# A two-block transformer forward on one core: an earlier query unit and halved ropes in mixer B, and narrow row sums for the norm ahead of the third FFN

## What is computed

```python
def mixer_b(h, cos16, sin16, w_in, sinks):
    q, k, v, q_mem = split_cols(h @ w_in, B_SPLITS)          # 1024, 256, 256, 256
    q = apply_partial_rope(q.reshape(B, S, 16, 64), cos16, sin16)
    k = apply_partial_rope(k.reshape(B, S, 4, 64), cos16, sin16)
    ...
    o, _ = banded_window_attention(q, k, v, 127, 64 ** -0.5, sink=sinks)
    return o.reshape(B, S, 1024), q_mem

# third layer, after its mixer
x = x + gt1 * rmsnorm_2(y, g_post1)
h2 = rmsnorm_2(x, g_pre2) * (1 + sc2) + sh2
x = x + gt2 * rmsnorm_2(conv_ffn(h2, ...), g_post2)
```

## Time and profile before

| what | value |
|---|---|
| median of 3 runs | 2167.69 us (2163.6 to 2168.49) |
| time of the profiled execution | 2167.15 us |
| its span in the trace | 2165.4 us |
| mean granted TensorE clock | 0.972 |
| mixer B: from the last projection matmul to the first output matmul | 827.0 to 967.9 us |
| post1 and pre2: from the last matmul of `c_out` to the first of `up20` | 1748.4 to 1783.1 us |

### The profile page before, as it was taken

The page is one execution under the profiler, slowest core; times in us unless marked ns, Lnnn a source line. Parts: engine busy times, 40 slices in busy tenths (PEclk is TensorE's granted clock), DMA queues, the critical chain, the costliest instruction groups (busy, mean ns, idle before and its releaser), DMA issues.

```text
span 2165.4 us, 25929 instructions
## 1 busy us (share of the span) xinstructions
PE 2001.3 (92%) x9702; PEld 1598.4 (74%) x9702; DVE 1122.4 (52%) x2007; ACT 670.7 (31%) x1058; POOL 871.2 (40%) x648
## 2 busy tenths in 40 slices
PE   3989789999999988989999999999999959999997
PEld 3766467788778776558788887788876848888886
DVE  7777874533943675754534534872233554312334
ACT  3233463321122124562321222234444222212211
POOL 4343103444744552105445544542221423444442
PEclk9999899999999999999999999999999979999998
DMA  4222001422532341003324422332110212223221
GB/s 159 78 79 97 25 1 63 165 98 73 209 136 91 139 150 59 25 23 110 117 91 149 160 97 104 104 105 76 59 59 20 98 57 79 85 80 117 97 80 66
DMA packets 32205, 199.14 MB, mean 92 GB/s; under 512 B 3696, under 2 KB 3824, under 8 KB 14320
## 3 DMA queue, kind: packets, MB, share of 16 engines
q1 hardware_dynamic: 27216, 166.74, 22.0%
q10 hardware_dynamic: 4896, 31.15, 4.0%
HBM read 195.78 MB, written 2.10 MB: 91 GB/s over the span
## 4 chain that ended last, share of the span: by engine, by line
PE 49%; DVE 4%; ACT 1%; POOL 1%; issue 1%; DVEq 0%; ACTq 0%
PE psum L1514 42%; PE psum L1536 2%; PE psum L1707 2%; PE psum L1689 1%; POOL w_lo L565 1%; PE psum L1672 1%; PE psum L1974 1%; DVE xT L1024 1%; DVE work L1018 1%; PE psum L1644 0%; ACT w_hi L595 0%; PE psum L1635 0%; DVE work L1029 0%; DVE h_lo L1008 0%; PE psum L1628 0%
## 5 line engine op out<-in xcount | busy, mean ns | idle before, releaser
L565 POOL TENSOR_TENSOR w_lo<-raw,w_hi 128x512 fp32r<-128x512 f32 (+2 forms) x640 | 862.7, 1376 | 1264.8 <-ACT w_hi L595 1264.8
L1514 PE MATMUL psum<-h_hi,w_hi 128*128 128x512 f32 x1560 | 614.2, 394 | 14.1 <-POOL w_lo L565 6.6
L1514 PE MATMUL psum<-h_hi,w_lo 128*128 128x512 f32 x1560 | 611.2, 392 | 0.0
L1514 PE MATMUL psum<-h_lo,w_hi 128*128 128x512 f32 x1560 | 610.5, 391 | 0.0
L595 ACT ACTIVATE w_hi<-raw 128x2048 fp32r<-128x2048 f32 (+3 forms) x177 | 301.6, 1704 | 565.7 <-PE psum L1514 474.4
L1514 PEld LDWEIGHTS psum<-h_hi,w_hi 128*128 128x128 f32 x1560 | 294.0, 188 | 87.4 <-issue 14.5
L1514 PEld LDWEIGHTS psum<-h_hi,w_lo 128*128 128x128 f32 x1560 | 293.7, 188 | 63.6 <-issue 2.4
L1514 PEld LDWEIGHTS psum<-h_lo,w_hi 128*128 128x128 f32 x1560 | 293.8, 188 | 62.2 <-issue 2.3
L1514 PE MATMUL psum<-g_hi,w_hi 128*128 128x512 f32 x528 | 207.6, 393 | 10.9 <-POOL w_lo L565 5.8
L1514 PE MATMUL psum<-g_hi,w_lo 128*128 128x512 f32 x528 | 205.6, 389 | 0.0
L1514 PE MATMUL psum<-g_lo,w_hi 128*128 128x512 f32 x528 | 205.6, 389 | 0.0
(11 more groups left out here) (312 smaller groups left out, 2424.1 us busy)
## 6 DMA issues: line engine op xcount, KB each, us to landing
raw<-w_up SPq DMA_DIRECT2D x66, 1024.0 KB, 4.8
raw<-w_dn SPq DMA_DIRECT2D x48, 704.0 KB, 4.1
mod_w<-w_mod ACTq DMA_DIRECT2D x24, 1024.0 KB, 4.9
raw<-w_c_in SPq DMA_DIRECT2D x13, 1024.0 KB, 4.9
raw<-w_b_in SPq DMA_DIRECT2D x7, 1024.0 KB, 4.9
raw<-w_a_idx SPq DMA_DIRECT2D x5, 1024.0 KB, 5.7
raw<-w_a_out SPq DMA_DIRECT2D x8, 640.0 KB, 3.9
raw<-w_b_out SPq DMA_DIRECT2D x8, 640.0 KB, 3.9
```

Of the source, the lines that this page charges most:

```text
L565: ins = nc.gpsimd.tensor_tensor(LO[slot][:, a:z], RAW[slot][:, a:z], HI[slot][:, a:z].bitcast(F32), ALU.subtract)
L1514: ins = nc.tensor.matmul(out, l, r, start=(k == 0 and m == 0), stop=(k == n - 1 and m == 2))
```

## The change

Mixer B: the unit of query tiles 0 and 1 comes second and the values third (the columns of the weight are laid out so). The start of attention on PE waits for keys and those two query tiles, no more for the values. At step 0 PE issues `AHEAD_B` = 12 filler matmuls ahead of the first transposes, and 6 a step from then on instead of 7; `b_finished` counts that. Ropes inside attention are halved: shuffle and times cosine in one step, times sine and add in the next. ACT evaluates one exponential before the projections, which brings its table in there.

Third FFN: `pre2` sums each square on PE with one moving column into banks 0 to 3, chunk by chunk, and puts its inverses into bank 5.

```diff
-          ("b_in", 7, 2048, [2, 4, 2, 2, 2, 2, 2]), ("b_out", 8, 1280, 1),
+          ("b_in", 7, 2048, [2, 2, 4, 2, 2, 2, 2]), ("b_out", 8, 1280, 1),
...
-        FILL_MEM, FILL_B, FILL_C, LAST_C = 12, 7, 40, 12
+        FILL_MEM, FILL_B, AHEAD_B, FILL_C, LAST_C = 12, 6, 12, 40, 12
+
+        def b_finished(k):
+
+            return (AHEAD_B + FILL_B * k) // 24 if k > 0 else 0
...
                 root, sums = T[:, 2, 0:rows], bank(norm_bank(name), 0, rows)
+                if name == "pre2":
+                    root, sums = ROOT[:], ps[:, 0:4 * S].rearrange("p (t n) -> p t n", n=S)[:, :, 0]
...
             for u in range(3):
                 next_hi(ph, u // 2, u % 2)
-                if u == 1:
+                if u == 0:
+                    nc.scalar.activation(WARM[:, 14:15], cst("eps"), ACT.Exp)
+                if u == 2:
                     for t in range(ROWT):
...
+                    elif name == "pre2":
+                        nc.vector.reciprocal(INV[:], ROOT[:]).then_inc(pre2_inverse, 1)
+                        v.wait_ge(pre2_spread, 1)
+                        inv = bank(5)
...
                 step(nc.vector.stream_shuffle(sw, src, mask))
+                if later:
+                    step(nc.vector.tensor_tensor(dst, src, cos[0:n, :], ALU.mult))
+
+                    def rest():
+                        step(nc.vector.tensor_tensor(sw, sw, sin[0:n, :], ALU.mult))
+                        nc.vector.tensor_tensor(dst, dst, sw, ALU.add).then_inc(done, 1)
+                    return rest
...
             def b_between(k):
-                for tile in range(min(finished(FILL_B, k - 1) if k else 0, 6), min(finished(FILL_B, k), 6)):
-                    b_tile(3 + tile // 2, tile % 2, BQ[:, 2 + tile, :], 5 + tile)
+                if begun:
+                    begun.pop()()
+                for tile in range(min(b_finished(k - 1), 6), min(b_finished(k), 6)):
+                    begun.append(b_tile(3 + tile // 2, tile % 2, BQ[:, 2 + tile, :], 5 + tile, later=True))
...
+                if name == "pre2":
+                    for t in range(ROWT):
+                        bank_free(t)
+                    for k in range(nch):
+                        pe.wait_ge(square_ready, b + k + 1)
+                        for t in range(ROWT):
+                            ins = nc.tensor.matmul(bank(t, 0, 1), T[:, k % 2, t * P:(t + 1) * P], ONES[:, 0:1],
+                                                   start=k == 0, stop=k == nch - 1)
+                        ins.then_inc(square_used, 1)
+                    bank_free(5)
+                    pe.wait_ge(pre2_inverse, 1)
+                    for t in range(ROWT):
+                        ins = nc.tensor.matmul(bank(5, t * P, (t + 1) * P), INV[:, t:t + 1].broadcast_to([P, P]),
+                                               cst("ident", P), start=True, stop=True)
+                    ins.then_inc(pre2_spread, 1)
...
-                if u == 1:
-                    last_read[4] = (scaled_ready, NORMS["mix1"][4] + DC)
+                if u == 2:
                     advance(r_tiles(ph, u, range(4), range(4, 8), 0, 256))
...
                     group = (k + 2) // 4
-                    if k % 4 == 2 and 2 <= group < 8:
+                    if k == 0:
+                        advance(rest, AHEAD_B)
+                    if k % 4 == 2 and group < 8:
                         pe.wait_ge(ph.free, 3 + group)
-                    elif k % 4 == 2 and group == 8:
-                        pe.wait_ge(qkv_ready, 15)
+                    elif k % 4 == 2 and group < 10:
+                        pe.wait_ge(qkv_ready, 6 + group)
                 else:
                     advance(rest, FILL_B)
-            pe.wait_ge(qkv_ready, 13)
-            pe.wait_ge(ph.free, 4)
+            pe.wait_ge(ph.free, 3)
```

More of the change, by code:

```diff
@@ L148, in lay_out @@
     bq = b[:, :1024].reshape(D, 16, 64)[:, pair16].reshape(D, 1024)
-    w["b_in"] = units(np.concatenate([b[:, 1024:1536], bq, b[:, 1536:]], 1), 256)
+    w["b_in"] = units(np.concatenate([b[:, 1024:1280], bq[:, :256], b[:, 1280:1536], bq[:, 256:], b[:, 1536:]], 1), 256)
     bo = x["b_w_out"][0]
@@ L370, in program @@
         final_inverse, final_spread = sem("final_inverse"), sem("final_spread")
+        pre2_inverse, pre2_spread = sem("pre2_inverse"), sem("pre2_spread")
         XR = {"final": 0, "post1": 8, "post2": 16}
@@ L882, in _ @@
                 next_hi(ph, u // 2, u % 2)
-                if u == 1:
+                if u == 0:
+                    nc.scalar.activation(WARM[:, 14:15], cst("eps"), ACT.Exp)
+                if u == 2:
                     for t in range(ROWT):
-                        act.wait_ge(ph.done, ph.before(1) + t + 1)
+                        act.wait_ge(ph.done, ph.before(2) + t + 1)
                         nc.scalar.activation(BV[:, t, :], bank(4 + t, 0, 256), ACT.Copy).then_inc(qkv_ready, 1)
@@ L889, in b_between @@
             def b_between(k):
-                for tile in range(min(finished(FILL_B, k - 1) if k else 0, 8), min(finished(FILL_B, k), 8)):
+                for tile in range(min(b_finished(k - 1), 8), min(b_finished(k), 8)):
                     if tile >= 6:
@@ L1039, in _, with rope @@
             ropes = []
-            def rope(src, dst, cos, sin, half, done, count, n=P, swapped=None, scale=1.0):
+            def rope(src, dst, cos, sin, half, done, count, n=P, swapped=None, scale=1.0, later=False):
                 if swapped == "bank":
@@ L1419, in _, with b_tile @@
             ph = PH["b_in"]
-            def b_tile(u, c, dst, count, scale=1.0):
+            def b_tile(u, c, dst, count, scale=1.0, later=False):
                 v.wait_ge(ph.done, ph.before(u) + c + 1)
-                rope(bank((u % 2) * 2 + c if u < 3 else c), dst, C16, S16, 8, ph.free, count, swapped=BSW, scale=scale)
+                return rope(bank(2 * u + c if u < 2 else c), dst, C16, S16, 8, ph.free, count, swapped=BSW, scale=scale, later=later)
             for c in range(2):
@@ L1427, in _ @@
             for c in range(2):
-                b_tile(2, c, BQ[:, c, :], c + 3)
+                b_tile(1, c, BQ[:, c, :], c + 3)
+            begun = []
             def b_between(k):
-                for tile in range(min(finished(FILL_B, k - 1) if k else 0, 6), min(finished(FILL_B, k), 6)):
-                    b_tile(3 + tile // 2, tile % 2, BQ[:, 2 + tile, :], 5 + tile)
+                if begun:
+                    begun.pop()()
+                for tile in range(min(b_finished(k - 1), 6), min(b_finished(k), 6)):
+                    begun.append(b_tile(3 + tile // 2, tile % 2, BQ[:, 2 + tile, :], 5 + tile, later=True))
             attend(b_all, b_between)
@@ L1613, in norm @@
                 i, nch, rows, b, s = NORMS[name]
+                if name == "pre2":
[13 more added lines that the diff above has]
+                    ins.then_inc(pre2_spread, 1)
+                    for t in range(ROWT):
+                        last_read[t] = (root_ready, i + 1)
+                    last_read[5] = (scaled_ready, s + nch)
+                    return
                 bank_free(norm_bank(name))
@@ L1864, in _ @@
                     advance(t_tiles(ph, u, (0, 1), (b, b + 1), ready=h_chunk("mix1") if u == 0 else None))
-                    last_read[b], last_read[b + 1] = (ph.free, u + 1), (ph.free, u + 2)
+                    last_read[b], last_read[b + 1] = (ph.free, 2 * u + 1), (ph.free, 2 * u + 2)
             def b_rest():
```

## The result

The changed kernel takes **2154.20 us** (median of 5 runs, 2152.42 to 2155.39), the kernel before 2167.69: a ratio of 0.994, 95% interval 0.9926 to 0.9955. That is 0.6% faster, with an interval that leaves out 1: the sign is as forecast, but the gain is 13.5 us instead of 21.4, and the time lies just above the upper end of the range (2153). The profiled execution took 2153.27 us, with a span of 2151.5, so 13.9 us less span than before.

The account below looks back on a forecast made before the run. PE was taken as the bound nearly everywhere, so only its idle and lower-clock time could go: 7.5 + 2.7 + 11.2 = 21.4 us off the profiled 2167.15 gives 2145.7 us, range 2138 to 2153.

Parts of the forecast that it names:

- Start of attention: Mixer B, projections' end to second transposes: idle and low-clock time of 9.2 us go, less new idle 1.7; gain 7.5 us.
- x: New PE idle time ahead of the first transposes in mixer B, put at 1.7 us.
- all-or-nothing bound of 3.6: Start of attention: if PE still falls to the lower clock, 3.6 us are lost again and 3.9 left.
- Three stalls: PE's waits before transposes inside mixer B: halved ropes cut them from 7.7 to 5.0 us, gain 2.7.
- rival 1: Stalls in mixer B: POOL holds up both instructions of the rope's second half, losing 1.9 us; 2147.6; chance 0.17.
- The rest of mixer B: Fillers lasting until step 30 instead of 27 shorten the bare steps at the end; nothing put on it.
- pre2: Third FFN: narrow sums beside post1 bring up20 12.4 us earlier, less 1.2 for its lower clock; gain 11.2.
- 2: Mixer B: half ropes fit DVE's slack whatever POOL does, no stalls left, 5.0 us less; 2140.7; chance 0.15.
- 3: Mixer B: with 6 fillers DVE and ACT can't follow, mixer B gives nothing, pre2 alone remains; 2156.0; chance 0.10.
- 5: pre2: a bank or buffer keeps narrow sums from running beside post1, 8.4 us follow the last update; 2151.2; chance 0.05.
- 4: Cold clock at the FFN's up20 and at attention's start, total gain only 9.5 us; 2157.6; chance 0.06.
- 6: Attention: thinner filler keeps PE at the lower clock, kernel slower, about 2236 over the whole stretch; chance 0.02.

Follow-up runs that it names:

- e5: Changed kernel with POOL writing only the first 64 columns of the low weights beside the three stalls (results partly wrong): 2142.38 us, one run.
- e6: Changed kernel with ACT's three weight copies inside attention one step later, behind that step's exponentials: 2143.71 us, one run.
- e4: Changed kernel with POOL writing four weight units in pieces of 128 columns instead of 512: 2144.07 us, one run.
- e1: Kernel before with the pre2 part of the change alone: 2157.37 us, ratio 0.9967.
- e7: Changed kernel with whole ropes, 7 fillers a step and none ahead of the first transposes: 2156.65 us, one run.
- e11: Changed mixer B with pre2's wide sums, root and reciprocal of before, the sums in free bank 5 instead of 4: 2154.86 us, one run.
- e12: Changed kernel with POOL pieces of 128 columns, ACT's copies one step later and extra unread matmuls around pre2: median 2140.68 us in two groups, ratio 0.9877.
- e2: Changed kernel with pre2 as before, so the mixer B part alone: 2161.82 us, ratio 0.9986.
- e3: Changed kernel with each rope in attention whole again, all else as changed: 2156.33 us, one run.

## Why the prediction was right or wrong

The sign, the two places and the additive sum were right. The forecast was 8.5 us too low against the median, 7.6 against the profiled execution; the stalls and pre2 missed by 3.3 us each, the start by 1.6. By terms, of the 21.4 forecast:

- **Start of attention, 7.5: mechanism right, a size off, 5.9.** No idle time ahead of the scores, and x = 1.72 for 1.7; that isn't luck, since line 1122 took 2.27 us beside POOL for the 2.20 assumed and the transposes came 6.24 us behind the projections for 6.3. The step "I take 7.5, since 12 fillers now stand where 4 us were idle" put the clock's loss at nothing. The row shows means of 0.80 and 0.82 over 9 us; I had priced this only as an all-or-nothing bound of 3.6, and it came to 1.6. The claim of "a granted clock above 0.9 from 827 to 840" failed.
- **Three stalls, 2.7: wrong, -0.6.** The failed step is "such a stall has two parts, the rope ahead of the maxima and DVE instructions that POOL holds up". The earlier trace rows had both before my eyes, and the rope did run there; but it ran beside ACT's copy of 1.91 us, which waits for the same tile of PE and stands ahead of the exponentials. A rope cut in half only lets DVE arrive earlier at a wait for ACT (the 1.14) and at POOL (1.25 for 0.15 on line 1118, in place of the add's 1.66): from the shuffle's start to the end of the probabilities it took 7.53 us before (860.46 to 867.99) and takes 7.23 now. That copy was in none of the prediction's terms for these stalls, though it was in the one for the start. POOL's part was priced at 1.6 for one instruction; it is 1.25 and 2.39 on two, where the same two take 0.15 and 0.62 in a step without POOL. e5, e6 and e4 show it. The Trainium skill's rule ("SBUF — State Buffer", "Who interferes with whom") that the later engine waits out the other's whole instruction agrees with the ends of POOL's instructions above and with e4; but it was used for rival 1, the second half of the rope, which started at 857.90, when POOL had ended.
- **The rest of mixer B, 0: -1.1.** The clock over the four microseconds behind the first two stalls is 0.67 and 0.63, where before it was 0.57 and 1.00, so 1.1 us more lost. Their length isn't what makes the difference: e1 and e7, with stalls of 3.15 and 3.24 as before, have 0.50 and 0.57, and 0.50 and 0.50. What sets it stays open, and this part of the comparison hangs on the one profile of the kernel before. The bare steps at the end won 0.9 (waits of 0.85 and 0.64 before, one of 0.63 now). The other 0.9 us lost are spread thin, and I can't name them.
- **pre2, 12.4 less 1.2: 9.1 less 0.6.** That the sums can run beside post1 was right, and e11 shows that nearly all of the gain is that (8.5 of 9.1). The failed step is "Eight narrow matmuls take 1.05 us, so PE keeps pace". The duration is of a row that ran at the upper level (a granted 1.00 from 1749.66 to 1751.00 in the kernel before); the earlier trace rows have the idle time in which PE would wait, and at the lower level the eight take 1.72, more than DVE's 1.38. That made the sums 3.2 us late and the spread 0.8; the way from scaling to matmul was 0.6 better than taken from mix1. I had weighed the lower clock for `up20` only, where little came of it (its first 48 matmuls took 13.7 us for 12.6 before), and not for the sums themselves, which had it for all of their 13.8 us; beside the wide ones of e11 it had a mean of 0.89 from 1754 on. The Trainium skill ("TensorE: Matmul & The Clock Gate", Part 1) says that the gate is set by how busy PE has been recently. By that alone the clock should have risen here, with PE busy in 13.76 of 13.80 us, and the trace does not agree: it stayed at 0.50. e12's N of 22.49 is near what the forecast's way would have given (26.0 less 3.4).
- **What no term had**: 2.1 us won ahead of mixer B and 0.8 lost behind it, in stretches whose work the change leaves as it was. The first is luck, by the range of 5 us above. Without both the profiled execution would have missed the forecast by 8.9 us instead of 7.6.

The rivals: 1 and 2 both took the rope to be the stall's heart and fell with it. 3 (steps as the bound, 2156.0) came nearest to the median and not in mechanism: e2 shows that mixer B does give something, and e3 that with whole ropes it would have been true. 5 had the right place, sums that end late, for a bank that was in fact free; they ended 4.9 us behind the last update, between the 1.7 forecast and its 8.4. 4 holds in part at the start. 6 didn't happen. One figure of the working doesn't follow from its source: 96 matmuls at half of 0.23 us are 11.0 us and not 11.5. The trace has them 0.12 apart, which is 11.5, and nothing hangs on it.

## What to carry to other kernels

A long instruction of GpSimd beside short ones of VectorE on the path can cost its whole rest each time. Here it did so for the sum of two tiles in SBUF (1.25 us for 0.15) and for the scaling of a tile by a number per partition (2.39 for 0.62), and not for the reciprocal (0.17). Cut it into pieces, and put a weight copy behind, not ahead of, the exponentials that others wait for; that gave more here (B 136.7 to 122.4) than the change of order. When a stall is split into causes, list everything that is released by the same event on every engine, and see which of them would be next once one is gone. And a matmul's duration holds for the clock level of its row: check which level the new place has before you write "keeps pace". Last, look at what the same code takes in several profiles before a stage's difference is called a gain: here one stretch ahead of the change moved by 5 us.

## What the hardware showed that was not expected

Narrow matmuls (128x1) without a gap do not bring the granted clock up: 0.50 over 13.78 us, PE busy in all of it. Wide ones at the same place had it at a mean of 0.89 in the second four microseconds. Nor did the narrow ones hold it once it was up: with one or two 128x512 matmuls between groups of eight it lasted three and six chunks.

A VectorE instruction on 128x2 numbers takes 1.25 us beside 512-column instructions of GpSimd and 0.46 beside 128-column ones; it isn't its size that sets this. The reciprocal of the same 128x2 numbers right behind it takes 0.17 in both. Cutting GpSimd's instructions to a quarter made a unit 1.54 times as long, 7.77 us for 5.04.
